# A hybrid decoder layer with 64 routed experts: 45 expert units in place of 50, with 96-slot experts beside quarters of split ones, and two weight loads asked for earlier

## The reference

```python
scores = sigmoid(x @ w_router); biased = scores + e_bias         # (520, 64)
# 4 of 8 groups by the sum of their two best, then the best 8 experts in them
wts = sel / sum(sel) * 2.5                                       # gates (T, 64), 8 of them not zero
a = silu(x @ w_gate[e]) * (x @ w_up[e])                          # 1024 -> 256, per expert
routed = sum over e of (a * gate[:, e]) @ w_down[e]              # 256 -> 1024
shared = (silu(x @ ws_gate) * (x @ ws_up)) @ ws_down
```

## Time and profile before

| | |
|---|---|
| median of 3 runs | 1336.12 us (1334.14 to 1341.52) |
| the profiled execution | 1335.09 us, span 1333.4 us, mean granted clock 0.948 |
| TensorE | 5832 products' passes |
| DMA, whole span | 457.72 MB, mean 343 GB/s |
| chain that ended last: TensorE | 67% of the span |
| ... of it, L750 (gate and up) and L774 (down) | 23% and 11% |

### The profile page before, as it was taken

One profiled execution on the slowest core, in us unless ns is written; L12 is line 12 of the kernel. 1 busy time (PEld: TensorE's weight loads), 2 busy tenths in 40 slices (PEclk: granted clock), 3 DMA queues, 4 the chain that ended last, 5 costly groups with the idle time before them and its releaser, 6 DMA issues.

```text
span 1333.4 us, 17713 instructions
## 1 busy us (share of the span) xinstructions
PE 1181.1 (89%) x5832; PEld 610.5 (46%) x5832; DVE 485.1 (36%) x1389; ACT 273.7 (21%) x612; POOL 244.7 (18%) x290
## 2 busy tenths in 40 slices
PE   3999999957787878999899999999899889899991
PEld 1687774324343335445344444444344334344340
DVE  2356457034443432345623222322222223223226
ACT  2232342123232224121111111111111111111110
POOL 0200000232333220000012222222122212222110
PEclk9999999989878888999999999999899989899896
DMA  9979999999999898999799999999999899999844
GB/s 370 421 285 347 333 369 332 341 361 350 391 326 388 334 377 303 359 312 383 253 382 330 354 386 387 383 383 356 387 347 387 305 391 360 349 341 369 306 148 145
DMA packets 92830, 457.72 MB, mean 343 GB/s; under 512 B 16040, under 2 KB 16584, under 8 KB 75968
## 3 DMA queue, kind: packets, MB, share of 16 engines
q1 hardware_dynamic: 59552, 347.80, 67.6%
q0 software_dynamic: 28912, 81.49, 19.6%
q10 hardware_dynamic: 4272, 27.27, 6.2%
HBM read 435.13 MB, written 106.77 MB: 406 GB/s over the span
## 4 chain that ended last, share of the span: by engine, by line
PE 67%; DMA 14%; DVE 6%; SPq 6%; issue 5%; ACT 1%; DVEq 0%; POOLq 0%
PE banks L750 23%; PE banks L774 11%; PE banks L1751 7%; DMA reg_w<-in_w_down 7%; PE banks L583 4%; PE banks L1741 4%; PE banks L737 3%; SPq L1576 2%; SPq L1577 2%; PE banks L645 2%; DMA reg_w<-in_cache_k 2%; DVE reg_s L2007 2%; PE banks L672 1%; PE banks L1918 1%; PE banks L1736 1%
## 5 line engine op out<-in xcount | busy, mean ns | idle before, releaser
L750 PE MATMUL banks<-reg_q,reg_w 128*128 128x512 f32 (+1 forms) x528 | 207.1, 623 | 19.5 <-issue 17.3
L750 PEld LDWEIGHTS banks<-reg_q,reg_w 128*128 128x128 f32 (+1 forms) x528 | 79.4, 174 | 141.8 <-issue 141.8
L1152 DVE SCALAR_TENSOR_TENSOR reg_w<-banks,small,reg_w 128x256 f32<-128x256 f32 x50 | 24.2, 484 | 314.5 <-ACT reg_w L1345 314.5
L774 PE MATMUL banks<-reg_q,reg_w 128*128 128x512 f32 (+1 forms) x324 | 132.7, 602 | 1.4 <-DMA reg_w<-in_w_down 0.9
L1498 POOL DMA_INDIRECT reg_w<-h_rows,gidx x50 | 51.9, 1039 | 410.1 <-DVE gidx L1113 353.3
L1502 POOL DMA_INDIRECT routed_sum<-reg_w,sidx x64 | 97.2, 1519 | 142.1 <-issue 75.9
L1345 ACT ACTIVATE reg_w<-banks 128x256 f32<-128x256 f32 x50 | 19.2, 384 | 442.5 <-PE banks L750 442.5
L1751 PE MATMUL banks<-hT,reg_q 128*128 128x260 f32 x384 | 88.3, 389 | 3.9 <-DVE spare L1973 2.3
L750 PE MATMUL banks<-hT,reg_w 128*128 128x512 f32 (+1 forms) x176 | 82.5, 624 | 0.0
L1751 PEld LDWEIGHTS banks<-hT,reg_q 128*128 128x128 f32 x384 | 73.6, 193 | 15.7 <-issue 4.3
L750 PE MATMUL banks<-spare,reg_w 128*128 128x512 f32 (+1 forms) x160 | 75.1, 625 | 6.0 <-issue 6.0
(11 more groups left out here) (378 smaller groups left out, 1573.6 us busy)
## 6 DMA issues: line engine op xcount, KB each, us to landing
reg_q<-in_w_gate_up SPq DMA_DIRECT2D x33, 2048.0 KB, 37.4
reg_q<-in_w_down SPq DMA_DIRECT2D x33, 1024.0 KB, 35.5
out_win_k_s<-in_win_k SPq DMA_DIRECT2D x8, 4094.0 KB
out_win_v_s<-in_win_v ACTq DMA_DIRECT2D x6, 4094.0 KB
reg_w<-in_w_ada SPq DMA_DIRECT2D x11, 2048.0 KB, 15.0
hT<-in_w_gate_up SPq DMA_DIRECT2D x11, 2048.0 KB, 37.7
spare<-in_w_gate_up SPq DMA_DIRECT2D x10, 2048.0 KB, 39.0
reg_s<-in_w_gate_up SPq DMA_DIRECT2D x10, 2048.0 KB, 43.9
```

What stands on the lines that cost most here:

```text
L750: last = mm(pb[j % 2][of, :], lhsT=xT[:, j % 2, k, of], rhs=wgu[LOAD[p] % NBUF][:, k, :], start=(k == 0), stop=(k == KC - 1))
L774: last = mm(pb[6 + hh][of, :], lhsT=aT[:, j % 2, c, of], rhs=down_w(LOAD[p] % NBUF, c, hh), start=(c == 0), stop=(c == 1))
```

## The change

`unit_table` makes three kinds of unit. Places 0 to 15 (`SOLO`) are alone. Places 16 to 35 have 96 slots (`WIDE`) each; in their unit the last 32 slots (`QUARTER`) belong to an expert of places 36 to 45, which is split: its slots 0 to 31 are worked on in one unit and 32 to 63 in the next, so two units share three experts. Places 46 to 63 go in pairs as before. That makes 16 + 20 + 9 = 45 units. A part of a unit is now (place, first column, number of columns, first slot), and `bands` cuts a part of 96 columns in one of 64 and one of 32, since the stationary operand's pieces are 32, 64 or 128 wide.

Scatters are counted by parts (`SENT`) and not by loads: there are 74. `onehot`, the index copy and `count_more` follow the new limits (128, 96 and 64 rows). On SP's queue, the down of buffer 5 and the gate-and-up of buffer 6 move ahead of buffer 4's two loads, behind the wait for the experts' table.

```diff
-    single = [(p,) for p in range(NB)]
-    pairs = [(p, p + 1) for p in range(NB, NE, 2)]
-    units, rest = single[:FIXED], single[FIXED:NB - LATE]
-    for n, two in enumerate(pairs):
-        units += rest[len(rest) * n // len(pairs):len(rest) * (n + 1) // len(pairs)] + [two]
-    return units + single[NB - LATE:]
+    single = [((p, 0, SLOTS, 0),) for p in range(SOLO)]
+    trios = []
+    for n, p in enumerate(range(SOLO, NB, 2)):
+        split = NB + n
+        trios.append([((p, 0, WIDE, 0), (split, WIDE, QUARTER, 0)), ((p + 1, 0, WIDE, 0), (split, WIDE, QUARTER, QUARTER))])
+    pairs = [((p, 0, HALF, 0), (p + 1, HALF, HALF, 0)) for p in range(NB + len(trios), NE, 2)]
+    units, rest = single[:FIXED], single[FIXED:SOLO - LATE]
+    for n, trio in enumerate(trios):
+        units += rest[len(rest) * n // len(trios):len(rest) * (n + 1) // len(trios)]
+        units += pairs[len(pairs) * n // len(trios):len(pairs) * (n + 1) // len(trios)] + trio
+    return units + single[SOLO - LATE:]
+def bands(first, n):
+    return [slice(first, first + n)] if n != WIDE else [slice(first, first + HALF), slice(first + HALF, first + WIDE)]
...
             def up(j):
...
                 for k in range(KC):
-                    for n, p in enumerate(UNITS[j]):
-                        of = part(n, UNITS[j])
-                        last = mm(pb[j % 2][of, :], lhsT=xT[:, j % 2, k, of], rhs=wgu[LOAD[p] % NBUF][:, k, :],
-                                  start=(k == 0), stop=(k == KC - 1))
+                    for p, first, n, _ in UNITS[j]:
+                        for of in bands(first, n):
+                            last = mm(pb[j % 2][of, :], lhsT=xT[:, j % 2, k, of], rhs=wgu[LOAD[p] % NBUF][:, k, :],
+                                      start=(k == 0), stop=(k == KC - 1))
...
             def count_more(r):
-                V.reduce_max(over_f[:, 0:1], cnt[:, 0:NB], AX.X).then_inc(route, 1)
-                V.reduce_max(over_f[:, 1:2], cnt[:, NB:NE], AX.X).then_inc(route, 1)
+                V.reduce_max(over_f[:, 0:1], cnt[:, 0:SOLO], AX.X).then_inc(route, 1)
+                V.reduce_max(over_f[:, 1:2], cnt[:, SOLO:NB], AX.X).then_inc(route, 1)
+                V.reduce_max(over_f[:, 2:3], cnt[:, NB:NE], AX.X).then_inc(route, 1)
...
             load_gu(4, I["w_gate_up"][LOADS[4]])
-            sp.wait_ge(sgu_ready, TT)
-            load_gu(3, I["w_gate_up"][LOADS[3]])
-            sp.wait_ge(sy_ready, 2 * TT)
-            load_dn(3, I["w_down"][LOADS[3]])
...
-            sp.wait_ge(experts_set, 1)
+            sp.wait_ge(experts_set, 2)
             sp.wait_ge(h2_set, TT)
             sp.wait_ge(h2_out[0], 16 * 3)
             sp.wait_ge(tables_placed, 3)
             load_dn(4, I["w_down"][LOADS[4]])
             gu_of(5)
+            sp.wait_ge(sgu_ready, TT)
+            load_gu(3, I["w_gate_up"][LOADS[3]])
+            sp.wait_ge(sy_ready, 2 * TT)
+            load_dn(3, I["w_down"][LOADS[3]])
             sp.wait_ge(x1_set, 4 * TT)
             dn_of(5)
```

More of the change, by code:

```diff
@@ L1 @@
+import itertools
 from contextlib import ExitStack
@@ L161 @@
 COUNT_AT = 4
-LOADS = [p for places in UNITS for p in places]
+LOADS = list(dict.fromkeys(p for parts in UNITS for p, _, _, _ in parts))
 NBUF = 6
 LOAD = {p: n for n, p in enumerate(LOADS)}
-UNIT = {p: j for j, places in enumerate(UNITS) for p in places}
+UNIT = {p: j for j, parts in enumerate(UNITS) for p, _, _, _ in parts}
+SENT = list(itertools.accumulate((len(parts) for parts in UNITS), initial=0))
+NSENT = SENT[NU]
 def into(n):
-    return n % 2 if n < NE - LATE else 0
+    return n % 2 if n < NSENT - LATE else 0
 def added(a, n):
@@ L539, in landed_sums @@
         def landed_sums(a, j):
-            return scattered[a], 16 * (ZEROS + added(a, LOAD[UNITS[j][-1]] + 1))
-        def part(n, places):
-            return slice(HALF * n, HALF * n + HALF) if len(places) == 2 else slice(0, SLOTS)
+            return scattered[a], 16 * (ZEROS + added(a, SENT[j + 1]))
         def row(v_, t, c0, n):
@@ L720, in ids @@
                     pe.wait_ge(tables_moved, 4)
-                for n, p in enumerate(UNITS[j]):
-                    of = part(n, UNITS[j])
-                    for t in range(TT):
-                        n_ = rows_of[t]
-                        last = mm(pb[5][of, 0:6], lhsT=oh[0:n_, t, of], rhs=comb[0:n_, t, p, :], start=(t == 0), stop=(t == QB))
+                for p, first, n, _ in UNITS[j]:
+                    for of in bands(first, n):
+                        for t in range(TT):
+                            n_ = rows_of[t]
+                            last = mm(pb[5][of, 0:6], lhsT=oh[0:n_, t, of], rhs=comb[0:n_, t, p, :], start=(t == 0), stop=(t == QB))
                 last.then_inc(id_ready, 1)
@@ L740, in up @@
             def up(j):
-                for p in UNITS[j]:
+                for p, _, _, _ in UNITS[j]:
                     pe.wait_ge(*gu_landed(LOAD[p]))
@@ L771, in down @@
                     for c in range(2):
[L772 to L775, removed]
+                        for p, first, n, _ in UNITS[j]:
+                            for of in bands(first, n):
+                                last = mm(pb[6 + hh][of, :], lhsT=aT[:, j % 2, c, of],
+                                          rhs=down_w(LOAD[p] % NBUF, c, hh), start=(c == 0), stop=(c == 1))
                     last.then_inc(y_ready, 1)
@@ L1096, in onehot @@
                     dve.wait_ge(id_ready, j)
-                for n, p in enumerate(UNITS[j]):
-                    wide = HALF if len(UNITS[j]) == 2 else SLOTS
+                for i, (p, first, n, base) in enumerate(UNITS[j]):
                     for t in range(TT):
                         n_ = rows_of[t]
-                        last = V.tensor_scalar(oh[0:n_, t, wide * n:wide * n + wide], slotno[0:n_, 0:wide], slot[0:n_, t, p:p + 1],
+                        last = V.tensor_scalar(oh[0:n_, t, first:first + n], slotno[0:n_, base:base + n], slot[0:n_, t, p:p + 1],
                                                None, ALU.is_equal)
-                        if t < QB or n + 1 < len(UNITS[j]):
+                        if t < QB or i + 1 < len(UNITS[j]):
                             last.then_inc(route, 1)
@@ L1186, in vector_after @@
                 if len(UNITS[j]) == 2:
-                    V.tensor_copy(sidx2[u][0:HALF, :], gidx1[a][HALF:SLOTS, :]).then_inc(sidx2_set, 1)
+                    _, first, n, _ = UNITS[j][1]
+                    V.tensor_copy(sidx2[u][0:n, :], gidx1[a][first:first + n, :]).then_inc(sidx2_set, 1)
                 if j + AHEAD < NU:
@@ L1190, in vector_after @@
                 if j == COUNT_AT:
-                    steps = r + sum(5 * len(places) - 1 for places in UNITS[:j + AHEAD + 1])
+                    steps = r + sum(5 * len(parts) - 1 for parts in UNITS[:j + AHEAD + 1])
                     dve.wait_ge(route, steps)
@@ L1203, in vector_after @@
             for n in range(2):
-                dve.wait_ge(scattered[n], 16 * (ZEROS + added(n, NE)))
+                dve.wait_ge(scattered[n], 16 * (ZEROS + added(n, NSENT)))
             dve.wait_ge(route_set, 1)
@@ L1217, in vector_after @@
                         j = i * NE + e
[L1218 to L1219 removed]
+                        dve.wait_ge(scattered[0], j * 16 + 16 * (ZEROS + added(0, NSENT)))
+                        dve.wait_ge(m_y, i * (NE + 1) + 3)
                         for t in range(TT):
@@ L1457, in sync_after @@
             sp.wait_ge(y_ready, 2 * (NU - LATE) + 2)
-            sp.wait_ge(scattered[1], 16 * (ZEROS + added(1, NE)))
+            sp.wait_ge(scattered[1], 16 * (ZEROS + added(1, NSENT)))
             for t in range(TT):
@@ L1519, in pool_after @@
                 pool.wait_ge(sidx_set, j + 1)
[L1520 to L1525, removed]
+                for i, (_, first, n, _) in enumerate(UNITS[j]):
+                    if i:
+                        pool.wait_ge(sidx2_set, sum(len(parts) - 1 for parts in UNITS[:j + 1]))
+                    a = into(SENT[j] + i)
+                    pool.wait_ge(scattered[a], 16 * (ZEROS + added(a, SENT[j] + i)))
+                    scatter(u, sidx2[u] if i else sidx1[u], a, slice(first, first + n))
             pool.wait_ge(route_set, 1)
@@ L1537, in pool_after @@
                         gather(0, gidx1[0], xg_in[0])
-                        pool.wait_ge(scattered[0], j * 16 + 16 * (ZEROS + added(0, NE)))
-                        pool.wait_ge(m_y, i * (NE + 1) + (e + 3))
+                        pool.wait_ge(scattered[0], j * 16 + 16 * (ZEROS + added(0, NSENT)))
+                        pool.wait_ge(m_y, i * (NE + 1) + (e + 4))
                         pool.sem_inc(asked, 1)
                         scatter(0, gidx1[0], 0)
-            pool.wait_ge(scattered[0], more * (16 * NE) + 16 * (ZEROS + added(0, NE)))
-            pool.wait_ge(scattered[1], 16 * (ZEROS + added(1, NE)))
+            pool.wait_ge(scattered[0], more * (16 * NE) + 16 * (ZEROS + added(0, NSENT)))
```

(1 more changed line is left out.)

16 lines of the change are left out of this document (12 added, 4 removed).

## The result

The changed kernel takes 1517.94 us (median of 4 runs, 1513.17 to 1520.21), the kernel before beside it 1336.22 us (4 runs, 1334.14 to 1341.52). The ratio is 1.1365, with a 95% interval of 1.133 to 1.140. The prediction was 1518 us. Its profiled execution has a span of 1511.4 us against 1333.4.

What follows compares the result with a forecast made beforehand. In the expert loop TensorE and DMA were both taken as nearly full, with TensorE setting the loop after the change. 1335 + 217 (TensorE) - 35 (late weights) = 1517, 1518 us on the median's scale; range 1485 to 1560.

Steps and rivals of the forecast that it cites:

- The step: Gate-and-up and down of a 96 + 32 unit: 64-piece 0.97 us, then two 32s 0.98, together 1.95 against a pair's 0.88.
- The assumption that had no row: 96 + 32 units on TensorE: pieces of different sizes wait for each other even on disjoint columns; otherwise about a pair's 12.6 us.
- the eleven that the prediction counts: Places in the before trace where 32-column products follow 64s back to back, starting 0.07 us ahead of the modelled end.
- TensorE's sum: Expert loop: units of one expert, pairs and 96 + 32 units take 818 us after, 601 before, 217 us more.
- late weights: Expert loop: 39 us lost before to late weights and the lower clock behind those waits; 35 given back, 4 staying.
- Number products: Slot numbers (`ids`) on TensorE in a 96 + 32 unit: 0.37 us more for a third band.
- The cover: VectorE's extra 15 us and GpSimd's 13 us lie beside TensorE's products, at nothing; thin if units were again 12.6 us.
- The moved loads: SP's queue: 3 MB start up to 19 us earlier; worth between 0 and 8 us, taken as 0.
- The first: Rival in 96 + 32 units: disjoint pieces overlap despite different sizes, TensorE needs 562 us, DMA decides; 1316 us, chance 0.13.
- The second: Rival in the expert loop: pieces overlap but DMA is already full, so nothing is won; 1333 us, chance 0.03.
- The third: Rival in the new units: drains also lower the granted clock from 1.0 to 0.9; 1575 us, chance 0.06.
- The fourth: Rival in the new units: serial without the extra 0.09 us, 1.72 us a step; 1463 us, chance 0.03.

Runs made afterwards that it cites:

- e1_all32: Changed kernel with every piece of a 96 + 32 unit cut to 32 columns: 1317.67 us, 0.9892 of the kernel before; again 1314.13 us, 0.9847.
- e4_pairs643232: Kernel before, with the second expert of each pair cut in two 32-column pieces in gate-and-up and down (64, 32, 32): 1477.98 us, ratio 1.1090.
- e2_sorted: Changed kernel, same three pieces, but all steps of the 64 before those of the 32s in gate-and-up and each half of down: 1468.7 us, ratio 1.1023.
- e9_all32_half_gu: e1_all32 with only the first half of each gate-and-up block fetched from the seventh load on: 1257.61 us, 0.9448 of the kernel before.
- e5_pairs32x4: Kernel before, with each expert of a pair cut in two 32-column pieces in gate-and-up and down: 1330.62 us, ratio 0.9985.

## Why the prediction was right

The mechanism is the one that was forecast: the two sizes take turns in each step, and a unit costs twice a pair. That 1518 us were predicted and 1517.94 measured is luck as far as the last few us go: the four runs lie 7 us apart, and two errors of the sum, of 2 and of 5 us, have opposite signs.

*The step.* Predicted 1.95 us, measured 1.99. The 0.04 us more is in the passes that begin a size: after a change the 64's first pass is 0.64 us long and its second starts 0.48 us behind it, where the prediction took 0.45 from a pair's start. The assumption that had no row, that disjoint columns don't help when the sizes differ, is now shown by the passes above, by e1_all32 and by e4_pairs643232. (The trace of before has twelve places where 32 columns follow 64 back to back, three at L1876 and nine at L1918, and not the eleven that the prediction counts; all have the 0.07 us.) The Trainium skill's sentence on it (TensorEngine Tiling (Array Packing), Tiling Modes, Key Properties: a change of the tiling mode drains TensorE) agrees with both: the next size starts 0.07 us ahead of the modelled end of the last pass, and e2_sorted shows 0.13 us for each such change.

*TensorE's sum.* A unit was put at 25.8 us and takes 25.9, so that the predicted 217 us more become 219. The stretch from the third unit's `up` to the last one's, 605.96 us in the kernel before, is 1467.28 - 682.48 = 784.80 us now, 178.8 more. The difference of 40 us to TensorE's own growth is what the kernel before had lost to late weights (39 us), and it came back entirely: TensorE is busy without a gap and at full clock from 700 to 1250 us. The prediction had given back 35; with the 2 us of the units these are the errors of the sum: 217 - 35 = 182 us predicted, 219 - 40 = 179 found, 178 between the two spans. Over the whole loop the changed kernel moves 268 GB/s, where the prediction worked out 270; only the DMA share is higher than its "near 0.7":

```profile
662.00:1480.00 818.00, 816.33 (x3147) 254.34 (x3147) 173.80 (x782) 83.15 (x178) 148.30 (x115) 1.00 0.77 268
```

*Number products.* Predicted 0.37 us more for the third band; the second row of the cycle above has 0.98 us for 15 against 0.74 for 10, 0.24 more.

*The cover.* VectorE and GpSimd stayed far from the path: 32.27 and 28.38 busy us of 150, less than the 44.80 and 37.65 of before, since the stretch holds fewer units. Where units are short again, in e1_all32, both carry more (64.68 and 62.87 of 250 us) and the end is still DMA's; the thin cover of the scatters that the prediction feared did not become the bound there: e9_all32_half_gu, with the same scatters, falls to the 1257 us (1257.61 measured) that it should have if TensorE's 562 us set the loop (its halved loads also leave the DMA engines freer for the scatters, so this is no proof for the full loads).

*The moved loads* were put at 0, between 0 and 8: no difference in either comparison, within intervals of some 4 us to each side.

*The rivals.* The first (overlap, 1316 us) did not happen in the changed kernel, but its sum was right for the kernel in which the pieces do overlap: e1_all32 took 1317.67 and 1314.13 us. The second (overlap, but nothing won) fell with the first, and where the pieces do overlap something is won: e1_all32's intervals end at 0.9955 and 0.9875. The third (a lower clock) is refuted by the granted clock of 1.00 in every stretch. The fourth (turns, but no drain, 1463 us) would be close to e2_sorted (1468.7 us), which had to remove most of the changes of size to get there.

## What to carry to other kernels

In these traces pieces of the array work side by side only while they have the same width: cut all pieces of a step to the smallest width in it, which costs nothing (0.9985 in e5_pairs32x4), or keep the widths in separate units. One mixed step cost 1.99 us here instead of 0.88. Before an engine's work is cut, look at what else is full: by the prediction's sums 39 us of TensorE's 601 are saved where the pieces overlap (562), and they are worth 15 to 20 us in e1_all32, since DMA is busy 0.95 to 1.02 of the loop. And a missing row (here: two widths on disjoint columns) is worth one small kernel of its own before the whole scheme is written: e4_pairs643232 changes a few lines.

## What was not expected

The median from issue to landing of a gate-and-up load into `reg_q` fell from 37.4 us in the kernel before to 10.9 us in the changed one:

```profile
reg_q<-in_w_gate_up SPq DMA_DIRECT2D x33, 2048.0 KB, 37.4
```

```profile
reg_q<-in_w_gate_up SPq DMA_DIRECT2D x33, 2048.0 KB, 10.9
```

The loads have the same size; what differs is the DMA share, 0.95 to 1.02 before and 0.75 to 0.82 after. So the landing time of a load here goes with how busy the DMA engines are and is not the time that the load takes by itself.

Sorting by size gives back only 2.4 of the 13.3 us by which a 96 + 32 unit (25.9 us) exceeds a pair (12.6 us). The larger part of the price is that a step's passes run in four turns where a pair's run in two; what each change of size costs on top of its turn is the smaller part. In the interleaved order the turns come from the sizes; in the sorted order it is open whether the sizes or the order of the products makes them.
